# 312 instead of 320 dense tokens: eight more are gathered, in one unit of sixteen slots on 64 partitions

## What is computed

```python
hin = rmsnorm(x) * (1 + sc1) + sh1
mix, state = token_mixers(hin, ...)     # gated MLP over chunks | bidirectional mLSTM -> concat -> w_out
x = x + g1 * mix
hin = rmsnorm(x) * (1 + sc2) + sh2
x = x + g2 * peer(hin, peer_wq, peer_keys, peer_u, peer_v)
```

```python
idx, gate = ...                          # (T, 8, 16): the chosen experts and the softmax of their scores
act = gelu(einsum('td,thkd->thk', tb, expert_u[ib]))
out = einsum('thk,thkd->td', gb * act, expert_v[ib])
```

## Time and profile before

| | |
|---|---|
| median of 3 runs | 3597.03 us (3596.15 to 3600.78) |
| the profiled execution's own time | 3590.64 us |
| its span | 3588.8 us |
| mean granted TensorE clock | 0.985 |
| TensorE busy | 97% of the span |
| VectorE, GpSimd, ScalarE busy | 75%, 54%, 17% |

### The profile page before, as it was taken

How to read it: one execution, slowest core, us unless ns; L and a number is a source line. 1 busy time by engine, 2 the same in 40 slices (tenths; PEclk the granted TensorE clock), 3 DMA queues, 4 the chain that set the end, 5 groups by cost and what they waited for, 6 DMA issues and landing times. The chain is left out here.

```text
span 3588.8 us, 46194 instructions
## 1 busy us (share of the span) xinstructions
PE 3465.2 (97%) x15864; PEld 2455.2 (68%) x15864; DVE 2691.0 (75%) x5792; ACT 592.7 (17%) x1241; POOL 1930.1 (54%) x1697
## 2 busy tenths in 40 slices
PE   7999999899999999999999999989999999999998
PEld 4554557877777777777766545677777777777776
DVE  3666989978777667666667788998878776766667
ACT  4222221710000000000032232144000000000001
POOL 0024536867656656556400363487765566655663
PEclk9999999999999999999999999989999999999999
DMA  9796674699999999999967476549999999999997
GB/s 371 265 358 237 254 270 133 196 382 410 410 410 405 410 410 409 410 410 409 387 239 228 164 279 234 197 138 305 410 409 410 410 407 409 410 409 409 410 410 292
DMA packets 447122, 1213.27 MB, mean 338 GB/s; under 512 B 36288, under 2 KB 165360, under 8 KB 446208
## 3 DMA queue, kind: packets, MB, share of 16 engines
q0 software_dynamic: 184320, 671.17, 47.9%
q1 hardware_dynamic: 258080, 535.06, 40.5%
q10 hardware_dynamic: 4576, 5.37, 0.4%
HBM read 1168.26 MB, written 42.55 MB: 337 GB/s over the span
## 5 line engine op out<-in xcount | busy, mean ns | idle before, releaser
L1300 PE MATMUL ps<-arena 128*128 128x320 f32 x4032 | 1130.1, 434 | 9.7 <-DMA arena<-in_peer_ut 8.4
L2683 POOL DMA_INDIRECT arena<-in_peer_u,arena x640 | 782.4, 1223 | 587.4 <-DVE act_c L2202 372.7
L2693 POOL DMA_INDIRECT arena<-in_peer_v,arena x640 | 746.3, 1166 | 538.5 <-DVE arena L2219 399.8
L1300 PEld LDWEIGHTS ps<-arena 128*128 128x128 f32 x4032 | 762.0, 191 | 290.1 <-issue 12.9
L2219 DVE SCALAR_TENSOR_TENSOR arena<-arena,wact 128x1024 f32<-128x1024 f32 x640 | 825.2, 1289 | 132.6 <-DMA arena<-in_peer_v,arena 127.8
L2202 DVE CUSTOM_DVE_ANT_0 arena<-arena 128x1024 f32<-128x1024 f32 x640 | 789.4, 1238 | 110.5 <-DMA arena<-in_peer_u,arena 107.4
L1313 PEld LDWEIGHTS ps<-arena 128*128 128x128 f32 x4096 | 680.0, 190 | 122.2 <-issue 122.2
L1313 PE MATMUL ps<-arena 128*128 128x192 f32 x4096 | 707.6, 327 | 0.0
L1308 PE MATMUL ps<-arena 128*128 128x512 f32 x1024 | 481.2, 593 | 0.0
L1701 ACT ACTIVATE arena<-ps 128x320 f32<-128x320 f32 x256 | 111.4, 436 | 1760.7 <-PE ps L1300 1760.6
L2529 DVE TENSOR_TENSOR arena<-arena 128x280 f32<-128x280 f32 x256 | 114.1, 446 | 363.9 <-PE ps L1313 352.8
(11 more groups left out here) (380 smaller groups left out, 2948.4 us busy)
## 6 DMA issues: line engine op xcount, KB each, us to landing
arena<-in_peer_ut SPq DMA_DIRECT2D x256, 512.0 KB, 6.8
arena<-in_peer_v SPq DMA_DIRECT2D x256, 512.0 KB, 7.4
arena<-in_w_mod SPq DMA_DIRECT2D x48, 1024.0 KB, 10.7
arena<-in_w_in SPq DMA_DIRECT2D x48, 1024.0 KB, 8.5
arena<-in_peer_wq SPq DMA_DIRECT2D x48, 1024.0 KB, 6.5
arena<-expert_gates SPq DMA_DIRECT2D x64, 560.0 KB, 8.8
expert_gates<-arena SPq DMA_DIRECT2D x12, 2560.0 KB, 10.2
arena<-in_w_out SPq DMA_DIRECT2D x16, 1024.0 KB, 8.9
```

Of the source, the lines that this page charges most:

```text
L1300: last = pe.matmul(bank(6 + par, 0, NX), u_s[par][:, k, :], h_d[:, k, X0:ND], start=(k == 0), stop=(k == KD - 1))
L2683: pool.indirect_dma_start(out=u_ring[U_PLACE[n]], out_offset=None, in_=io["peer_u"][:, :], in_offset=bass.IndirectOffsetOnAxis(ap=rows_at( ...
L2693: pool.indirect_dma_start(out=v_ring[V_PLACE[n]], out_offset=None, in_=io["peer_v"][:, :], in_offset=bass.IndirectOffsetOnAxis(ap=rows_at( ...
```

## The change

Eight more dense tokens are gathered: X0 = 64 + 8, NX = 312, MOVED = 184, 39 groups of gates instead of 40 (seven blocks of 40 tokens as before, the last of 32 in `gate_k`). The eight tokens times eight heads are one more unit of sixteen slots on 64 partitions (a partition is one token and one head), placed after the 64 tokens' units. Its gathers, dots and additions have 64 partitions. OPS becomes 672, QE 112, so 560 operations are left for the steps instead of 562. The labels ahead of the steps are finer (m0c, m0d, ..., n0). The eight rows go to DRAM and back, and 8 x 3 small DMAs spread choices, gates and rows over the partitions, ahead of the wait on s_qd; a second fold (`fold_c`) adds the unit's partial sums.
ScalarE takes from VectorE the gMLP value squares, the head squares, norm2's squares and the other half of norm2's scaling. The heads' scaling and addition (two operations on 512 and 256 columns) become two tensor_scalar and two scalar_tensor_tensor on 128 columns each.

```diff
-X0 = XB
+XF = 8
+X0 = XB + XF
...
-KEPT = NX // BLOCKS
-GW = NX - KEPT
+KEPT = 40
+GW = KEPT * (BLOCKS - 1)
+LAST = NX - GW
...
-ROUNDS = (0, PH, PH + P // PARTS // TOPK, 2 * PH + P // PARTS // TOPK)
+ROUNDS = (0, PH, PH + P // PARTS // TOPK, PH + P // PARTS // TOPK + 1, 2 * PH + P // PARTS // TOPK + 1)
...
-LABELS = ("p0", "p1", "p2", "p3", "g0", "g1", "g2", "c0", "c1", "c2", "m0a", "m0b", "m1a", "m1b", "m2a", "m2b", "m3a", "m3b", "n", "h0", "h1", "h2", "h3")
+LABELS = ("p0", "p1", "p2", "p3", "g0", "g1", "g2", "c0", "c1", "c2", "m0a", "m0c", "m0b", "m0d", "m1a", "m1c", "m1b", "m1d", "m2a", "m2c", "m2b", "m2d", "m3a", "m3c", "m3b", "m3d", "n0", "n", "h0", "h1", "h2", "h3")
 EARLY = [dict(zip(LABELS, counts)) for counts in (
-    (0, 4, 9, 13, 15, 18, 25, 31, 32, 36, 36, 39, 42, 45, 48, 51, 54, 58, 63, 69, 72, 75, 78),
-    (4, 8, 12, 16, 18, 20, 26, 31, 32, 36, 36, 39, 42, 45, 48, 51, 54, 58, 63, 69, 72, 75, 78))]
+    (0, 2, 7, 12, 14, 17, 21, 28, 35, 37, 42, 44, 47, 50, 53, 55, 58, 61, 64, 66, 69, 72, 75, 77, 80, 83, 86, 92, 97, 102, 107, 112),
+    (4, 9, 14, 19, 22, 26, 32, 37, 39, 43, 45, 47, 50, 53, 55, 57, 60, 63, 65, 67, 70, 73, 75, 77, 80, 83, 86, 92, 97, 102, 107, 112))]
...
+                    for part in range(PARTS_F):
+                        at, slots = slice(XF * part, XF * (part + 1)), slice(TOPK * part, TOPK * (part + 1))
+                        sp.dma_start(idx_f[at, 0, :], idx_a[XB:X0, 0, slots]).then_inc(s_qd, 16)
+                        sp.dma_start(gate_f[at, 0, :], exp_gate[XB:X0, 0, slots]).then_inc(s_qd, 16)
+                        sp.dma_start(row_f[at, :], rows_kept).then_inc(s_qd, 16)
+                    sp.wait_ge(s_qd, 16 * (2 * PARTS + 3 * PARTS_F))
...
+                        for n in range(KD):
+                            last = pe.matmul(turned(n, XB, X0), row_f[0:PF, n * P:(n + 1) * P], fold_c[0:PF, :],
...
+                    act.wait_ge(s_pe, 2 * ST)
+                    act.activation(flat(og), flat(vs), ACT.Square).then_inc(s_vsq, 1)
...
                         act.wait_ge(s_m2, t + 1)
-                        act.activation(ss2[:, t:t + 1], ss2[:, t:t + 1], ACT.Sqrt).then_inc(s_q2, 1)
+                        act.activation(xn[t % 2], x_s[:, t, :], ACT.Square, accum_out=ss2[:, t:t + 1]).then_inc(s_sq2, 1)
+                        act.wait_ge(s_sq2, t + 1)
+                        act.activation(ss2[:, t:t + 1], ss2[:, t:t + 1], ACT.Sqrt, bias=spare[:, 0:1], scale=1.0 / D).then_inc(s_q2, 1)
...
-                        act.activation(ss5[:, 4 * t:4 * t + 4], ss5[:, 4 * t:4 * t + 4], ACT.Sqrt).then_inc(s_r5, 1)
+                        act.wait_ge(s_hd, 2 * t + 2)
+                        for h in range(HEADS):
+                            act.activation(junk[:, h, :], hm[:, h * DH:(h + 1) * DH], ACT.Square, accum_out=ss5[:, 4 * t + h:4 * t + h + 1]).then_inc(s_hs, 1)
+                        act.wait_ge(s_hs, HEADS * (t + 1))
+                        act.activation(ss5[:, 4 * t:4 * t + 4], ss5[:, 4 * t:4 * t + 4], ACT.Sqrt, bias=spare[:, 0:1], scale=1.0 / DH).then_inc(s_r5, 1)
...
-                        lane.do(dve.tensor_tensor(h4[:, :, :, 0:DH], h4[:, :, :, 0:DH],
-                                                  den[:, 1, 0:4].rearrange("p (h d) -> p h d", d=2).unsqueeze(3).broadcast_to([P, 2, 2, DH]), ALU.mult))
-                        lane.settle()
-                        lane.do(dve.tensor_tensor(hm[:, 2 * x * DH:(2 * x + 2) * DH].rearrange("p (h e) -> p h e", e=DH),
-                                                  h4[:, :, 0, 0:DH], h4[:, :, 1, 0:DH], ALU.add), s_hd)
+                        for i in range(2):
+                            lane.do(dve.tensor_scalar(h4[:, i, 1, 0:DH], h4[:, i, 1, 0:DH], den[:, 1, 2 * i + 1:2 * i + 2], None, ALU.mult))
+                        lane.settle()
+                        for i in range(2):
+                            last = dve.scalar_tensor_tensor(out=hm[:, (2 * x + i) * DH:(2 * x + i + 1) * DH], in0=h4[:, i, 0, 0:DH],
+                                                            scalar=den[:, 1, 2 * i:2 * i + 1], in1=h4[:, i, 1, 0:DH], op0=ALU.mult, op1=ALU.add)
...
-                        for h in range(HEADS):
-                            lane.do(dve.tensor_tensor_reduce(out=junk[:, h, :], in0=hm[:, h * DH:(h + 1) * DH], in1=hm[:, h * DH:(h + 1) * DH],
...
-                        if t >= 2:
-                            scale2(t - 2)
+                        early(f"m{t}c")
```

More of the change, by code:

```diff
@@ L310, in build @@
         gate_s = [view(at, N_KEYS, KEPT) for at in (W, PW)]
+        gate_k, row_f = view(PW, N_KEYS, LAST), view(PW + N_KEYS * LAST, D)
+        idx_f, gate_f = view(QK + 1792, 1, TOPK, dt=U32), view(QK + 1792 + TOPK, 1, TOPK)
         u_s = [h_l, view(W + 3 * WSLOT, KD, P)]
@@ L540, in build @@
             GROUPS = DENSE * (P // OCT) - SKIPPED
-            UNIT = [(i, u - ROUNDS[i]) for i in range(3) for u in range(ROUNDS[i], ROUNDS[i + 1])]
+            UNIT = [(i, u - ROUNDS[i]) for i in range(4) for u in range(ROUNDS[i], ROUNDS[i + 1])]
+            turn_at = lambda i: 8 if i else max(8, SKIPPED)
             TAIL = (CTX, LATE, 2, 1, 0)
@@ L1282, in _ @@
                         i, g = (n + SKIPPED) // 16, (n + SKIPPED) % 16
-                        if g == 8 and i + 1 < DENSE:
+                        if g == turn_at(i) and i + 1 < DENSE:
                             choices(i + 1)
@@ L1634, in _ @@
                             norm2_rows(t - 1)
-                        early(f"m{t}b")
+                        early(f"m{t}d")
                     act.wait_ge(s_n2, ST - 1)
-                    norm2_scale(ST - 2, 2, range(4))
+                    norm2_scale(ST - 2, 2, range(KD))
                     norm2_rows(LATE)
@@ L2194, in _ @@
                     done = [0]
-                    row_of_round = (row_c, row_p, row_3)
+                    row_of_round = (row_c, row_p, row_f, row_3)
+                    held = (P, P, PF, P)
                     def dot(u, k):
@@ L2386, in out @@
                         lane.do(dve.tensor_tensor(x_s[:, t, sl], x_s[:, t, sl], xn[t % 2][:, sl], ALU.add))
-                    def squares(t):
-                        lane.settle()
-                        lane.do(dve.tensor_tensor_reduce(out=xn[t % 2], in0=x_s[:, t, :], in1=x_s[:, t, :], scale=1.0, scalar=0.0,
-                                                         op0=ALU.mult, op1=ALU.add, accum_out=ss2[:, t:t + 1]))
-                        lane.settle()
-                        lane.do(dve.tensor_scalar(ss2[:, t:t + 1], ss2[:, t:t + 1], 1.0 / D, EPS, ALU.mult, ALU.add), s_m2)
+                        if half == 1:
+                            lane.settle()
+                            dve.engine_nop().then_inc(s_m2, 1)
                     def reciprocal2(t):
@@ L2399, in reciprocal2 @@
                         lane.do(dve.reciprocal(rs2n[:, t:t + 1], ss2[:, t:t + 1]), s_v5)
-                    def scale2(t):
-                        dve.wait_ge(s_n2, t + 1)
-                        for k in range(4, KD):
-                            lane.do(dve.tensor_scalar(h_d[:, k, t * P:(t + 1) * P], bank(3, (k - 4) * P, (k - 3) * P),
-                                                      mod[:, 32 + k, 0:1], mod[:, 24 + k, 0:1], ALU.mult, ALU.add), s_hb)
                     dve.wait_ge(s_grl, 16)
@@ L2435, in _ @@
                             out(t - 1, 1)
-                            squares(t - 1)
+                        early(f"m{t}b")
+                        if t >= 1:
                             reciprocal2(t - 1)
-                        early(f"m{t}b")
+                        early(f"m{t}d")
                     out(LATE, 0)
-                    scale2(ST - 2)
                     out(LATE, 1)
-                    squares(LATE)
+                    early("n0")
                     reciprocal2(LATE)
```

99 lines of the change are left out of this document (55 added, 44 removed).

## The result

The changed kernel takes 3712.91 us (median of 4 runs, 3710.06 to 3714.47) against 3596.59 us for the kernel before in the same session: 3.2% slower, ratio 1.0323, 95% interval 1.031 to 1.0336. I had forecast 3598 us, in a range of 3577 to 3619. The profiled spans differ by 3708.3 - 3588.8 = 119.5 us.

What follows compares the result with a forecast made beforehand. TensorE, busy 97% of the span, was taken as the bound, with the DMA engines full but not late. Terms -53.9 + 3.7 + 18.2 + 1.4 + 31.3 = +0.7 us on 3597.03 gave 3598 us, range 3577 to 3619.

Steps and rivals of the forecast that it cites:

- Time here goes with bytes: DMA in the steps: half-height gathers cost by their bytes, 438 MB or 1068 us a layer, so no stretch.
- rival C: Steps: a half gather takes the engines as long as a full one; +26 us, 3623 us; chance 0.10.
- The small DMAs, 0.38 us apiece: SyncE before the steps: 24 more small DMAs delay u(4) by 9.1 us a layer, +18.2 us.
- rival B: Small DMAs cost 0.64 us each and VectorE's heads keep their stall; +22 us, 3619 us; chance 0.22.
- Ahead of the steps, +31.3: Before the steps: 112 gathered operations instead of 78, less ScalarE's help; +31.3 us, between 11 and 48.
- The mixing's operations: States to last mixed rows: 42 and 38 gathered operations instead of 22 add 23.6 and 18.9 us of VectorE.
- ScalarE's help: Mixing: squares and scaling taken from VectorE save 11.0 us, 15 us in all with the heads' stall.
- the heads' stall: Mixing: L2373 takes 0.43 us but once 4.13 beside GpSimd; most of this was counted as gone.
- The term for the states: gMLP rows to the states' last updates: more gathered operations there cost +4.7 and +0.5 us.
- It still fits, barely.: DMA in the steps: 438 MB take 1068 us at 410 GB/s, within 1072 us of steps.
- 0.21 us a step: TensorE's steps: 256 fewer columns save 0.216 us a step, -53.9 us over both layers.
- the fold: In the steps: a second set of eight blocks of records costs +1.8 us a layer, +3.7 us.

Runs made afterwards that it cites:

- e1: The changed kernel with the new unit's gathers fetching 128 rows instead of 64: 3644.46 us, ratio 1.0138 to the kernel before.
- e9: The kernel before with one unit's 32 gathers a layer fetching 64 rows instead of 128: 3664.26 us, ratio 1.0189.
- e2: The changed kernel with each of the new unit's gathers split into two of 32 rows, onto partitions 0 to 31 and 64 to 95: 3680.1 us.
- e3: The changed kernel with each of the new unit's gathers split into two of 32 rows, onto partitions 0 to 31 and 32 to 63: 3712.04 us.
- e10: The kernel before with one unit's 32 gathers a layer fetching 32 rows instead of 128: 3594.17 us, ratio 0.9998.
- e13: The kernel before with the changed kernel's 112 operations ahead of the steps and VectorE's old work: 3674.85 us, ratio 1.0224.
- e5: The kernel before with only ScalarE's part of the change (squares, scaling, heads) and 78 operations ahead of the steps: 3592.31 us, ratio 0.999.
- e11: The kernel before with u(4) and v(2) loaded ahead of SyncE's wait and 72 operations ahead of the steps instead of 78: 3603.53 us, ratio 1.0019.
- e7: The changed kernel with the eight tokens in eight slots on 128 partitions, five DMAs through DRAM, u(4) and v(2) ahead of the wait: 3603.39 us, ratio 1.0024.

## Why the prediction was wrong, point by point

Against the forecast's columns above, the miss of 119 us is 58.8 us in steps 60 to 74, 25.9 in steps 100 to 122, 16.9 at the start of the steps, 14.7 ahead of them, and some 3 in the other rows.

- **"Time here goes with bytes" (rival C's refusal).** This step failed, and it is more than half of the miss of 119 us: 58.8 us in steps 60 to 74, and by e1 68 us with what follows later. The sum counted a 64-row gather as 0.64 us of DMA, by its bytes. It costs 2.3 (e9). Rival C had the right place and the wrong size: it let a half gather cost as much as a full one, 1.28 us, for +26 us in all. I gave it 0.10. The rows of before had nothing on half the partitions, so bounding the price by bytes and by a full gather was a choice; the true price lay above both, and the measured time above the range and rival C's 3623. The Trainium skill, "SBUF — State Buffer", section "Door 1: The DMA port swizzle", says that DMA's rate depends on how many of sixteen ports the partitions reach, and that partitions 0 to 63 reach eight. The prediction did not weigh it. e2 against e3 agrees that reaching both sides helps, by 0.5 us for each pair of gathers. An estimate by that rule, 64 rows at half of 410 GB/s, is 1.28 us; the measurement is 2.3, so the rule gives the direction and not the size. That section of the Trainium skill also says that 64 partitions get about the bandwidth of 32. This agrees: 0.262 MB in 2.3 us and 0.131 MB in at most 1.25 us (e10) are 114 and at least 105 GB/s.
- **The small DMAs, 0.38 us apiece.** Mis-sized: 0.63 us, 15.15 us a layer in place of 9.1, nearly rival B's 0.64. The price should have come from L728 and L729, the same kind of transfer from SBUF to SBUF (0.60), and not from their size. The 18.0 us of the second layer are then these 15.15, the landing (5.57 instead of 4.53), the group less (2 us, saved ahead and waited away here, as forecast) and some 0.5 us of cold scores, less 0.7 us for u(4)'s own load (9.68 instead of 10.40). The number of partitions does not set the price: L741 over 64 partitions took 0.60 us, L745 over eight 0.64, and L746, over eight too but from DRAM, 0.46.
- **Ahead of the steps, +31.3.** Measured +46.0, within its bound of 48. The mixing's operations cost what I said (23.6 forecast, 102.3 - 78.4 = 23.9 in e13). ScalarE's help was 11.7 and 11.4, the 11.0 that I had summed, and not the 15 for which I counted the heads' stall. The new form of the heads does not remove it: the long execution moves. In e5 one tensor_scalar of the heads takes 4.46 us in the mixing of each layer; in the changed kernel the new heads' operations stay at 0.35 us and below, but L2400 takes 4.31 us in the second layer's mixing, and in the first layer's none takes over 2.9. What decides where it falls is not shown. The term for the states was mis-sized: +9.4 and +7.5 in place of 4.7 and 0.5. From the mixing's end to the steps it was +5.9 and +4.4, with the group less, instead of 6.8; but VectorE was hardly the bound of the routing with 78 operations: in e11 six fewer shorten that stretch by 2.8 and 2.5 us, not by 7. The heads' tensor_scalar in e5 (ns, least, median and most) and the long execution in the changed kernel:

```profile
L2378 DVE TENSOR_SCALAR arena<-arena,den x32: 280/289/4460, 393.8 to 2214.0; 128x128 f32<-128x128 f32 x32
```

```profile
2218.31 4.31 DVE L2400 SCALAR_TENSOR_TENSOR den<-arena 128x4 f32<-128x4 f32 x1
```

- **"It still fits, barely."** The 438 MB of a unit at its bytes would have fitted: e7 has them, and steps of 1080 and 1083 us for 1072. With the half gathers it did not. Of the 25.9 us in steps 100 to 122, 15.9 stay in e1, whose 446 MB are over what 1072 us of steps can carry at 410 GB/s, and none in e7.
- **Right:** 0.21 us a step, -53.2 us measured; the fold, +2.0 us in the first layer; that the group of gates less gains nothing, since TensorE's wait takes the place of what is saved ahead of it.

Open: why 64 rows on one side cost 1.8 times as much as 128 rows on both (2.3 and 1.28 us), and why a pair of 32-row gathers on the two sides still costs 1.8 us (2.3 - 0.5). Gathers onto partitions 64 to 127, and one gather of 64 rows across both sides, were not tried.

## What to carry to other kernels

Where DMA runs at its ceiling, a transfer has to be priced by where it lands, not by its bytes alone; let every gather cover all partitions, and if there are too few rows, take fewer gathers of full height. A kernel with TensorE at 97% can have DMA at its bound too: six gathers moved into the steps cost their full time. And work taken off an engine is worth something only when other work is put in its place: the same ScalarE part gave 3 us with 78 operations ahead and, with finer places for them, some 32 with 112.

## What the runs showed of the hardware

A gather of 64 rows of 4 KB onto partitions 0 to 63 cost the DMA engines 2.3 us, one of 128 rows 1.28, one of 32 rows at most 1.25: estimates from the GB/s lines of e9 and e10 at the 410 GB/s of full gathers. During one-sided gathers the engines' share stays at 1.03 while the rate falls to 266 GB/s, so the share doesn't tell that a transfer goes badly; the GB/s line does. Full-height loads beside them slow down too: 8.24 MB took 48.7% of the engines' time, where 8.52 MB took 35.7%. Two 32-row gathers on one side and on both sides, with equal bytes, differ by 32 us over 64 pairs, 0.5 us a pair.
